# Who rounds the weight pieces during two attentions: GpSimd, or ScalarE one piece per round

## The reference, cut to what matters

```python
def even_layer(x, mem, norm_g, w_in, qk_g, sinks, mem_norm_g, w_mem_kv, w_out):
    h = rms_norm_2(x, norm_g)
    aq, ak, av, bq, bk, bv, mq, z = split_cols(h @ w_in, EVEN_SPLIT)
    ...
    ya = sliding_window_sink_attn(aq, ak, av, sinks, slopes[:A_Q_HEADS])
    yb = moba_attn(bq, bk, bv, slopes[A_Q_HEADS:])
    ym = memory_cross_attn(mq, mk, mv)
    y = jnp.concatenate([ya, yb, ym], axis=-1) * jax.nn.silu(z)
    return x + y @ w_out
```

## Time and profile before

| | us |
|---|---|
| median of 3 runs | 1189.46 |
| lowest, highest | 1186.88, 1189.74 |
| the execution that was profiled | 1189.16 |
| its span, first to last instruction | 1187.4 |
| TensorE busy | 1160.2 (98%) |
| VectorE busy | 631.5 (53%) |
| ScalarE busy | 567.2 (48%) |
| GpSimd busy | 140.8 (12%) |
| granted TensorE clock, mean | 0.996 of 2.4 GHz |

### The profile page before, as it was taken

One profiled execution on the slowest core, in us unless ns is written; L12 is line 12 of the kernel. 1 busy time (PEld: TensorE's weight loads), 2 busy tenths in 40 slices (PEclk: granted clock), 3 DMA queues, 4 the chain that ended last, 5 costly groups with the idle time before them and its releaser, 6 DMA issues.

```text
span 1187.4 us, 15306 instructions
## 1 busy us (share of the span) xinstructions
PE 1160.2 (98%) x6002; PEld 950.1 (80%) x6002; DVE 631.5 (53%) x1171; ACT 567.2 (48%) x1012; POOL 140.8 (12%) x154
## 2 busy tenths in 40 slices
PE   6999999999999999999999999899999999999998
PEld 5887888888877777888788887677789788888877
DVE  5584423588434355524547663777445565167631
ACT  5443431233434545633236575777424576377720
POOL 1000000000000000000000005234323000513522
PEclk9999999999999999999999999999999999999999
DMA  5323223323321221332434233212223233222221
GB/s 186 126 75 103 84 93 111 107 73 105 124 89 46 79 89 36 123 107 88 175 110 107 79 99 81 62 36 72 48 95 109 71 107 99 71 72 76 77 72 71
DMA packets 107936, 107.89 MB, mean 91 GB/s; under 512 B 17932, under 2 KB 93068, under 8 KB 107864
## 3 DMA queue, kind: packets, MB, share of 16 engines
q1 hardware_dynamic: 106216, 100.69, 27.6%
q10 hardware_dynamic: 1648, 6.23, 1.4%
HBM read 104.64 MB, written 2.25 MB: 90 GB/s over the span
## 4 chain that ended last, share of the span: by engine, by line
PE 92%; DVE 4%; ACT 3%; issue 1%; DMA 0%; DVEq 0%; ACTq 0%
PE acc L1537 23%; PE acc L1539 23%; PE acc L1538 23%; PE aux L1717 3%; PE aux L1896 3%; PE acc L1864 3%; PE aux L1884 3%; PE aux L1537 2%; PE aux L1703 2%; PE aux L1539 2%; PE aux L1538 2%; DVE wlo L1011 1%; ACT whi L649 1%; PE aux L1766 0%; PE aux L1765 0%
## 5 line engine op out<-in xcount | busy, mean ns | idle before, releaser
L1537 PE MATMUL acc<-ht_hi,whi 128*128 128x512 f32 x736 | 292.0, 397 | 4.9 <-DVE wlo L1011 3.0
L1539 PE MATMUL acc<-ht_hi,wlo 128*128 128x512 f32 x736 | 286.5, 389 | 0.0
L1538 PE MATMUL acc<-ht_lo,whi 128*128 128x512 f32 x736 | 286.5, 389 | 0.0
L1011 DVE TENSOR_TENSOR wlo<-raw,whi 128x2048 fp32r<-128x2048 f32 x70 | 160.2, 2289 | 135.3 <-ACT whi L649 128.8
L1537 PEld LDWEIGHTS acc<-ht_hi,whi 128*128 128x128 f32 x736 | 138.2, 188 | 35.8 <-DVE wlo L1011 5.1
L594 POOL TENSOR_SCALAR whi<-raw 128x512 fp32r<-128x512 f32 x68 | 46.7, 687 | 991.2 <-DMA raw<-e_w_in_dram 737.8
L1538 PEld LDWEIGHTS acc<-ht_lo,whi 128*128 128x128 f32 x736 | 138.3, 188 | 29.7 <-issue 1.9
L1539 PEld LDWEIGHTS acc<-ht_hi,wlo 128*128 128x128 f32 x736 | 138.1, 188 | 28.9
L649 ACT ACTIVATE whi<-raw 128x2048 fp32r<-128x2048 f32 x70 | 133.6, 1911 | 50.8 <-DMA raw<-w_in_dram 23.3
L595 POOL TENSOR_TENSOR wlo<-raw,whi 128x512 fp32r<-128x512 f32 x68 | 88.7, 1305 | 5.7
L1537 PE MATMUL acc<-whi,ht_hi 128*128 128x512 f32 (+1 forms) x224 | 84.1, 375 | 0.8 <-DVE gbT L1261 0.8
(11 more groups left out here) (222 smaller groups left out, 1834.8 us busy)
## 6 DMA issues: line engine op xcount, KB each, us to landing
raw<-w_in_dram SPq DMA_DIRECT2D x72, 512.0 KB, 4.6
raw<-o_w_in_dram SPq DMA_DIRECT2D x28, 512.0 KB, 4.7
raw<-e_w_in_dram SPq DMA_DIRECT2D x14, 512.0 KB, 5.0
raw<-w_proj_pool_dram SPq DMA_DIRECT2D x8, 512.0 KB, 4.1
raw<-w_proj_mlstm_dram SPq DMA_DIRECT2D x8, 512.0 KB, 4.1
raw<-w_out_dram SPq DMA_DIRECT2D x8, 512.0 KB, 4.3
raw<-o_w_out_dram SPq DMA_DIRECT2D x8, 512.0 KB, 4.7
raw<-e_w_in_dram SPq DMA_DIRECT2D x14, 256.0 KB, 3.9
```

What stands on the lines that cost most here:

```text
L1011: v.tensor_tensor(wlo[:, slot, :], raw[:, slot, :], whi[:, slot, :].bitcast(F32), ALU.subtract).then_inc(w_split, 1)
L1537: mm(out_, w_hi_, x_hi, start=first, stop=False)
L1538: mm(out_, w_hi_, x_lo, start=False, stop=False)
L1539: return mm(out_, w_lo_, x_hi, start=False, stop=last)
```

## The change

The units z 0 to 3 and output 0 of both layers (ten in all, 40 pieces) are listed in `HI_BY_SCALAR`. For them GpSimd no longer rounds: it waits for a new semaphore, `w_hi_piece`, piece by piece, and subtracts. ScalarE does the rounding with `activation(..., Copy)` on 128 x 512. It does the four pieces of z unit 0 in a row ahead of round 0, and one piece at the end of every round: rounds 0 to 3 for z unit 1, 4 to 7 for z unit 2, 8 to 11 for z unit 3, and 12 to 15 for output unit 0. The other GpSimd units (output 1 to 3, and the ones elsewhere) stay as they were.

```diff
+        PIECES = 4
+        HI_BY_SCALAR = []
+        for name in "eo":
+            HI_BY_SCALAR += [plan[name + "_z"][0] + u for u in range(4)] + [plan[name + "_out"][0]]
...
-                for c in range(0, SLOT, SLOT // 4):
-                    piece = slice(c, c + SLOT // 4)
-                    step(nc.gpsimd.tensor_scalar(whi[:, slot, piece], raw[:, slot, piece], 1.0, 1.0, ALU.mult, ALU.mult))
+                for q in range(PIECES):
+                    piece = slice(q * (SLOT // PIECES), (q + 1) * (SLOT // PIECES))
+                    if n in HI_BY_SCALAR:
+                        pool.wait_ge(w_hi_piece, PIECES * HI_BY_SCALAR.index(n) + q + 1)
+                    else:
+                        step(nc.gpsimd.tensor_scalar(whi[:, slot, piece], raw[:, slot, piece], 1.0, 1.0, ALU.mult, ALU.mult))
                     ins = nc.gpsimd.tensor_tensor(wlo[:, slot, piece], raw[:, slot, piece],
                                                   whi[:, slot, piece].bitcast(F32), ALU.subtract)
...
+                def head_piece(i):
+
+                    n, q = HI_BY_SCALAR[5 * L + i // PIECES], i % PIECES
+                    piece = slice(q * (SLOT // PIECES), (q + 1) * (SLOT // PIECES))
+                    act.wait_ge(w_loaded[n % SLOTS], loaded(n))
+                    nc.scalar.activation(whi[:, n % SLOTS, piece], raw[:, n % SLOTS, piece], ACT.Copy).then_inc(w_hi_piece, 1)
+                for q in range(PIECES):
+                    head_piece(q)
+
                 def probabilities_of(p):
...
                     if i < NQ:
                         normalised(2 * i)
                         probabilities_of(2 * i + 1)
+                        head_piece(PIECES + i)
```

More of the change, by code:

```diff
@@ L210, in hybrid_block_then_two_attention_layers @@
         w_split_pool = sem("w_split_by_pool")
+        w_hi_piece = sem("w_hi_piece_by_scalar")
         acc_ready = sem("acc_ready")
```

## The result

| | before | changed |
|---|---|---|
| median of 5 runs, us | 1189.46 | 1198.66 |
| lowest, highest | 1186.88, 1190.66 | 1196.43, 1199.42 |
| ratio, 95% interval | | 1.0083, 1.0068 to 1.0098 |
| span of the profiled execution | 1187.4 | 1197.5 |

The account below looks back on a forecast made before the run. TensorE, busy for 98% of the span, was taken as the bound, so only its waits count. First attention +3.4 and second +5.6 gave +9.0 us on 1189.16: 1198.2 us, range 1192.0 to 1202.2.

Parts of the forecast that it names:

- Part 1: At each attention's start, TensorE waits for z unit 0, rounded too late: 4.9 us in the first, 3.9 in the second.
- Part 2: Behind those two waits TensorE's clock falls to its lower level, costing 1.3 us in the first attention, 1.7 in the second.
- Part 3: First attention's rounds: minima and copy waits -1.7, round 4 +1.2, round 6 -0.8 and its slow stretch -1.7; attention +3.4 us.
- Part 4: Second attention has no gate waits to give back, so it pays stall and clock in full: +5.6 us.
- Part 5: ScalarE's pieces in the rounds, z units 1 to 3, output units and SyncE's transfers cost nothing.
- more late units: Rival: round 4 brings a slow stretch, z unit 1 and both output units 0 come late; +3.9, 1202.1 us, chance 0.15.
- relief: Rival: less GpSimd port use frees VectorE, so first-attention waits and slow stretches go, 8.8 us; 1189.2 us, chance 0.06.

Follow-up runs that it names:

- e1: Changed kernel with z unit 0 of both attentions split wholly by GpSimd again; 1186.92 us, ratio 0.9981 to the kernel before.
- e2: Kernel before with only z unit 0 of both attentions rounded by ScalarE, in four pieces ahead of round 0; 1200.65 us, ratio 1.0100.
- e3: Changed kernel with 18 (first attention) and 14 (second) further matmuls on TensorE ahead of its wait for z unit 0; 1194.61 us, ratio 1.0050 to the kernel before.
- e6: Kernel before with only z unit 3 rounded by ScalarE, one piece at the end of each of rounds 8 to 11; 1183.96 us, ratio 0.9964.
- e5: Changed kernel with z unit 0 rounded between ScalarE's copies of values, other pieces two by two behind even rounds; 1183.34 us, ratio 0.9955 to the kernel before.
- e4: Changed kernel with ScalarE rounding z unit 0 between its copies of values; 1185.27 us, ratio 0.9979 to the kernel before.

## Why the prediction was right

The time, 1198.66 against 1198.2, follows from its own steps: the waits that it named came where it said. That it fits to 0.5 us is in part luck. The spans of the two profiles differ by 10.1 us and not 9.0, and in the first attention errors of about 1 us cancelled (parts 2 and 3).

*Part 1, late z unit 0.* Predicted waits 4.9 and 3.9 us, measured 4.67 and 3.65. Of the difference of 0.2 in the first attention, 0.1 is that ScalarE issued the first piece at 738.96, before the last copy ended at 739.06, so that GpSimd started 0.66 us behind that end and not 0.73; the other 0.1 is that the four subtractions took 4.94 us together and not 5.08. e1 and e2 show that this unit alone makes the loss.

*Part 2, the clock.* This is the term that was mis-sized. I took 1.3 and 1.7 us, with 1.7 as the upper bound, since each stretch in the earlier trace rows lasted 3.4 us. Behind the long stalls the low clock lasted 6.8 us, and by e3 it cost 2.5 and 2.4. It is the reason that the second attention is +6.3 and not +5.6. The bound was taken from waits of 1.7 to 1.8 us, and does not hold for the waits of 3.7 and 4.7.

*Part 3, the first attention.* The lag of TensorE against the kernel before, from the first logits on, was 5.6 us at the gate of round 2 (predicted 4.4, the difference again the clock), then +1.0 at round 4 (+1.2), -1.2 at round 6 (-0.8), and another 1.6 less by round 8, where the low clock behind round 6 is missing (-1.7). It ended at 3.5 against 3.4. GpSimd won between the two bias instructions in every even round from 2 to 10, as the rows at 723 had said. The pairs took 1.64 to 1.82 us where 1.8 to 2.2 was expected. The sum came out because errors cancelled, which is luck: the clock took 1.2 more, while round 4 took 0.2 less, and round 6 and the rounds behind it gave 0.4 and some 0.5 more back than assumed. The gate of round 8 had enough room, so its 0.3 was not paid. One reading was weak: the 1.1 us wait that was said to bring no low clock ended at 750.87 in the kernel before, only 5 us ahead of a low stretch, so it proves nothing. The changed kernel's wait of 1.20 in round 4, with no low clock behind it, is the clean case.

*Part 4, nothing given back in the second attention.* Right: there is no wait but the stall and the one for values.

*Part 5, edits at nothing.* Right. z units 1 to 3 and output unit 0 were waited for nowhere, although the latter had no reserve by my sum. The rival "more late units" did not come, nor did "relief"; the relief itself is real (e6 shows 4 us of it, low clock included), but it needs no rounding of z unit 0 by ScalarE.

## What to carry to other kernels

Before work is moved to an idle engine, ask where in that engine's order it will stand, and when it is wanted: here an engine busy half of the time came too late by 4 us, with idle time of its own just ahead. Then ask which instructions of a third engine the remaining work will now meet; a subtraction of 1.27 us beside the biases ahead of a gate that TensorE waits for cost 1.0 us, and one round later (e5) it cost nothing there, though ScalarE's two pieces in a row cost 0.4. And add to a stall the low clock that goes with it: here 3.4 us of it at most for waits of up to 2 us, and 6.8 for those of 3.3 us and more.

## What the runs showed of the hardware

The low clock lasted 6.8 us with stalls of 4.7 and 3.7 us, in the changed kernel and in e2 alike, and with e2's wait of 3.28. Of the eight waits of 1.7 to 1.9 us for the gate in the first attention, five brought 3.4 us (before 1.72 and 1.82, changed 1.85, e3 1.85, e4 1.86) and three brought none (e1 1.86 and e6 1.94 in round 2, e2 1.69 in round 6). Which of the two comes is not explained by these runs. Matmuls whose results nobody reads were enough to keep it up (e3).
VectorE's instructions with two operands in SBUF, and its bias pair, mostly stood still until a running instruction of GpSimd was over, however small they were (a sum of two columns, 1.27 us in e2). Not always: at 751.90 in the kernel before such a sum took 0.16 us beside a subtraction that had started less than 0.01 us earlier. GpSimd got in between two VectorE instructions that stand back to back in all five bias pairs from round 2 to round 10 of the changed kernel. The Trainium skill, "SBUF — State Buffer", section "Who interferes with whom", describes such a lock, held for a whole instruction; the rows agree with it, but for that one sum.
